# First mLSTM head of a hybrid encoder: its running maxima reach all partitions by transfers from DRAM, in place of products, a mask and copies

## What is computed

```python
b = jnp.cumsum(lfc, axis=-1)                               # log forget gates
dmat = jnp.where(tril, b[..., :, None] - b[..., None, :] + igc[..., None, :], -jnp.inf)
m_inter = b + m[..., None]
m_comb = jnp.maximum(jnp.max(dmat, axis=-1), m_inter)      # running maximum, the stabiliser
w_ts = jnp.exp(dmat - m_comb[..., None]) * jnp.einsum("bhtk,bhsk->bhts", qc, kc)
scale = jnp.exp(m_inter - m_comb)
num = jnp.einsum("bhts,bhsv->bhtv", w_ts, vc) + scale[..., None] * jnp.einsum("bhtk,bhvk->bhtv", qc, C)
den = jnp.sum(w_ts, axis=-1) + scale * jnp.einsum("bhtk,bhk->bht", qc, n)
h = num / jnp.maximum(jnp.abs(den), jnp.exp(-m_comb))[..., None]
```

## Time and profile before

| | before |
|---|---|
| median of 3 runs | 1865.18 us (1865.14 to 1869.9) |
| profiled execution, its own time | 1865.81 us |
| its span in the trace | 1864.0 us |
| granted TensorE clock, mean | 1.00 |
| PE busy | 1849.1 us, 99% |
| PE weight loads | 1741.0 us, 93% |
| VectorE | 1232.4 us, 66% |
| ScalarE | 880.2 us, 47% |
| GpSimd | 1161.8 us, 62% |
| SyncE's DMA queue | 349472 packets, 237.81 MB, 42.1% of 16 DMA engines |

### The profile page before, as it was taken

The page is one execution under the profiler, slowest core; times in us unless marked ns, Lnnn a source line. Parts: engine busy times, 40 slices in busy tenths (PEclk is TensorE's granted clock), DMA queues, the critical chain, the costliest instruction groups (busy, mean ns, idle before and its releaser), DMA issues.

```text
span 1864.0 us, 31419 instructions
## 1 busy us (share of the span) xinstructions
PE 1849.1 (99%) x10833; PEld 1741.0 (93%) x10833; DVE 1232.4 (66%) x2069; ACT 880.2 (47%) x1854; POOL 1161.8 (62%) x1533
## 2 busy tenths in 40 slices
PE   8999999999999999999999999999999999999999
PEld 8888888999999999999988888888889999999998
DVE  6756566768666766566866666666587575756663
ACT  6444343455444444455434444444465454444553
POOL 4543544468677878688843333333558788887885
PEclk9999999999999999999999999999999999999999
DMA  8789997549688877873466666654233535353534
GB/s 269 245 244 231 225 257 178 179 106 233 206 218 256 227 235 209 258 231 117 109 138 121 136 124 124 129 114 95 68 92 111 150 97 156 101 153 102 153 112 132
DMA packets 380153, 309.51 MB, mean 166 GB/s; under 512 B 14395, under 2 KB 322398, under 8 KB 379766
## 3 DMA queue, kind: packets, MB, share of 16 engines
q1 hardware_dynamic: 349472, 237.81, 42.1%
q0 software_dynamic: 28416, 69.21, 20.5%
q10 hardware_dynamic: 2134, 0.82, 0.2%
HBM read 302.16 MB, written 144.04 MB: 239 GB/s over the span
## 4 chain that ended last, share of the span: by engine, by line
PE 90%; DVE 6%; ACT 2%; issue 1%; DMA 1%; POOL 0%; ACTq 0%; DVEq 0%; SPq 0%; POOLq 0%
PE ps L974 50%; PE ps L884 26%; PE ps L1150 3%; PE ps L1307 3%; PE ps L1275 2%; PE ps L1297 1%; PE ps L1125 1%; DVE rstd L1497 1%; PE ps L1209 1%; PE ps L1159 1%; DVE sx L1549 0%; PE ps L1239 0%; DVE gt L1656 0%; PE ps L1027 0%; PE ps L1107 0%
## 5 line engine op out<-in xcount | busy, mean ns | idle before, releaser
L974 PE MATMUL ps<-sx,wh 128*128 128x400 f32 (+1 forms) x2044 | 530.4, 340 | 0.9 <-POOL wl L808 0.5
L808 POOL TENSOR_TENSOR wl<-raw,wh 128x256 fp32r<-128x256 f32 (+1 forms) x432 | 355.2, 853 | 99.7 <-ACT wh L2236 98.3
L774 POOL CAST wh<-raw 128x256 fp32r<-128x256 f32 x248 | 102.1, 453 | 454.2 <-PE ps L884 429.4
L974 PEld LDWEIGHTS ps<-sx,wh 128*128 128x128 f32 x2044 | 373.4, 188 | 2.8 <-ACT gt_first L2251 0.9
L974 PE MATMUL ps<-sx,wl 128*128 128x400 f32 (+1 forms) x1022 | 347.6, 340 | 0.0
L808 POOL TENSOR_TENSOR wl<-raws,wh 128x256 fp32r<-128x256 f32 x328 | 282.6, 906 | 82.8 <-ACT wh L2236 82.4
L1710 DVE TENSOR_TENSOR h<-h,ps 128x400 f32<-128x400 f32 (+1 forms) x280 | 154.5, 559 | 131.4 <-PE ps L974 131.2
L974 PE MATMUL ps<-fx,wh 128*128 128x400 f32 (+1 forms) x904 | 235.3, 341 | 0.1
L884 PE MATMUL ps<-xh,wh 128*128 128x512 f32 (+1 forms) x752 | 211.2, 357 | 0.0
L884 PE MATMUL ps<-xl,wh 128*128 128x512 f32 (+1 forms) x752 | 207.3, 349 | 0.0
L778 POOL TENSOR_TENSOR wl<-raw,wh 128x256 fp32r<-128x256 f32 x248 | 199.0, 831 | 5.1
(11 more groups left out here) (330 smaller groups left out, 3548.4 us busy)
## 6 DMA issues: line engine op xcount, KB each, us to landing
in_sums<-in_ffn_w_in_dram SPq DMA_DIRECT2D x16, 1536.0 KB, 10.6
raw<-in_sums SPq DMA_DIRECT2D x96, 256.0 KB, 3.1
in_sums<-in_ffn_w_in_dram SPq DMA_DIRECT2D x16, 1280.0 KB, 7.5
raw<-in_ffn_w_in_dram SPq DMA_DIRECT2D x80, 256.0 KB, 3.0
raws<-in_sums SPq DMA_DIRECT2D x80, 256.0 KB, 3.0
raw<-out_sums SPq DMA_DIRECT2D x120, 128.0 KB, 2.5
raws<-in_ffn_w_in_dram SPq DMA_DIRECT2D x52, 256.0 KB, 3.2
raw<-in_m_w_in_dram SPq DMA_DIRECT2D x24, 512.0 KB, 4.6
```

The source lines that it names most:

```text
L774: ins = pool.tensor_copy(wh[:, slot, c], raw[:, slot, c])
L808: ins = pool.tensor_tensor(slot_of(n, 1)[:, c], raw_of(n)[:, c], slot_of(n, 0)[:, c].bitcast(F32), ALU.subtract)
L974: mm = pe.matmul(product_bank(layer, s, j), slot_of(n, low_w)[:, k * P:(k + 1) * P], x, start=(j in OPENS and k + q == 0), stop=(k == tile ...
```

## The change

Head 0's maxima go the way of the others. The store is unchanged; behind it SyncE waits for its landing and issues the two broadcast reads of head 0 at once (`spread_maxima(0)`). The mask, the four products, ScalarE's two copies and their three semaphores are removed. VectorE waits for `maxima_in` 32 where it waited for `mrep_ready`, and for head hd in 1 to 3 on 32 more than before. `turn_ce` waits only for `gate_e`.

```diff
--- before.py
+++ after.py
@@ -523,7 +523,6 @@
         norm_sum, norm_root, rstd_ready = sem("norm_sum"), sem("norm_root"), sem("rstd_ready")
         vstep, astep, ones_set = sem("vstep"), sem("astep"), sem("ones_set")
         gates_done, gate_x, gate_soft, gate_m, gate_e = (sem(n) for n in ("gates_done", "gate_x", "gate_soft", "gate_m", "gate_e"))
-        mrow_masked, mrep_done, mrep_ready = sem("mrow_masked"), sem("mrep_done"), sem("mrep_ready")
         maxima_stored, maxima_in = sem("maxima_stored"), sem("maxima_in")
         ce_turned, ce_kept, ce_ready = sem("ce_turned"), sem("ce_kept"), sem("ce_ready")
         v_turned, vn_ready = sem("v_turned"), sem("vn_ready")
@@ -696,15 +695,19 @@
             sp.wait_ge(gate_m, 1)
             for d in range(2):
                 sp.dma_start(maxima_kept[d], mrow[64 * d:64 * d + M_HEADS, :]).then_inc(maxima_stored, 16)
+
+            def spread_maxima(hd):
+                for d in range(2):
+                    sp.dma_start(wk[:, 2 + d, :], maxima_kept[d, hd:hd + 1, :].to_broadcast([P, T])).then_inc(maxima_in, 16)
+
+            sp.wait_ge(maxima_stored, 32)
+            spread_maxima(0)
             for hd in range(1, M_HEADS):
                 for j in range(6):
                     n = MIX0 + hd * 6 + j
                     if j == 3:
-                        sp.wait_ge(maxima_stored, 32)
                         sp.wait_ge(e_ready, hd * NT)
-                        for d in range(2):
-                            sp.dma_start(wk[:, 2 + d, :], maxima_kept[d, hd:hd + 1, :].to_broadcast([P, T]))\
-                              .then_inc(maxima_in, 16)
+                        spread_maxima(hd)
                     weights(n, j % 2, mlstm_cols(hd, j))
                     sum_copies(n)
             for j in range(2):
@@ -1082,17 +1085,7 @@
 
             def mlstm_head(hd, n, first=False, last=False):
 
-                def repeat_m():
-
-                    pe.wait_ge(mrow_masked, 1)
-                    for d in range(2):
-                        for half in range(2):
-                            mm = pe.matmul(ps[:, 4 + 2 * d + half, 0:HT], ones[64 * d:64 * d + 32, :],
-                                           wk[64 * d:64 * d + 32, 4, half * HT:(half + 1) * HT], start=True, stop=True)
-                    mm.then_inc(mrep_done, 1)
-
                 def turn_ce():
-                    pe.wait_ge(mrep_ready, 2)
                     pe.wait_ge(gate_e, 2)
                     for i, (_, t0, tz) in enumerate(TILES):
                         mm = pe.transpose(flat(2)[0:tz, i * P:(i + 1) * P], cerow[:, t0:t0 + tz], ident)
@@ -1166,7 +1159,7 @@
 
                 run_block(n + 1, 1, 1, tokens="shared")
                 run_block(n + 2, 0, 0, tokens="shared")
-                run_block(n + 3, 1, 1, tokens="shared", between={2: [repeat_m], 4: [turn_ce], 7: call(turn_v, 0)} if first else {4: call(turn_v, 0)})
+                run_block(n + 3, 1, 1, tokens="shared", between={4: [turn_ce], 7: call(turn_v, 0)} if first else {4: call(turn_v, 0)})
                 tiles = {j + 2: call(scores, j) for j in OF_SEQ[0]}
                 tiles = {0: call(turn_v, 1), **tiles}
                 run_block(n + 4, 0, 0, tokens="shared", between=tiles)
@@ -1860,10 +1853,6 @@
 
                 if not first:
                     evacuate_shared(n, 0, wk[:, 0, :])
-                else:
-                    ve.wait_ge(gate_m, 1)
-                    ve.tensor_scalar(wk[:, 4, :], mrow[:, :], cst[:, ONEHOT:ONEHOT + 1], None, ALU.mult)\
-                      .then_inc(mrow_masked, 1)
                 evacuate_shared(*((n + 2, 0, wk[:, 6, :]) if first else (n + 1, 1, wk[:, 1, :])))
 
                 def query_key_lows():
@@ -1884,7 +1873,7 @@
                                          mask[0:tz, 0:tz], ALU.add).then_inc(diag_ready, 1)
 
                 if first:
-                    ve.wait_ge(mrep_ready, 2)
+                    ve.wait_ge(maxima_in, 32)
                     for j in (0, 1):
                         diagonals(j)
 
@@ -1900,7 +1889,7 @@
                 ve.tensor_copy(ce[:, :, :], ce_all[:, :, :, bass.ds(hd, 1)].rearrange("p i g c -> p i (g c)"))\
                   .then_inc(ce_ready, 1)
                 if not first:
-                    ve.wait_ge(maxima_in, hd * 32)
+                    ve.wait_ge(maxima_in, hd * 32 + 32)
                 for j in OF_SEQ[0][2 if first else 0:]:
                     diagonals(j)
                 if not first:
@@ -2543,10 +2532,6 @@
                 if not first:
                     query_key_high(n, 0)
                     query_key_high(n, 1)
-                else:
-                    sc.wait_ge(mrep_done, 1)
-                    for d in range(2):
-                        sc.activation(two(wk[:, 2 + d, :]), pair(2 + d), ACT.Copy).then_inc(mrep_ready, 1)
 
                 def values():
                     sc.wait_ge(v_turned, hd + 1)
```

## The result

The changed kernel takes 1872.22 us (median of 8 executions, 1871.36 to 1873.49), the kernel before beside it 1867.4 (8, 1865.14 to 1869.9). The ratio is 1.0029, 95% interval [1.002, 1.0037]: about 5.4 us slower, by the difference of the two medians 4.8. The forecast was 1872.0.

The account below looks back on a forecast made before the run. TensorE was taken to bound the kernel, with 90% of the last chain. Removing 1.55 us but adding a round trip, a 5.9 us stand and half clock gave +6.8 on the 1865.18 median: 1872.0 us, range 1867.0 to 1874.5.

Parts of the forecast that it names:

- case A: Stores wait behind the copy, PE stands near 6 us, clock falls: +6.2 to +7.3 us, chance 0.60.
- What it removes: Four products on PE's chain, 1.55 us; the VectorE multiply and ScalarE copies are off the chain, worth nothing.
- Step 1: On SyncE's queue: the maxima stores, issued at 56.15 behind the FFN weight copy, are done at 63.0.
- Step 2: SyncE issues the two spreads at 63.05 and 63.45; the second lands 5.1 us after issue, at 68.6.
- Step 3: VectorE makes four masked tiles (0.8 us) and the `ce_all` copies (0.5); PE starts `turn_v(0)` at 70.0.
- Steps 4 and 6: VectorE finishes block 3's evacuation at 72.2; ScalarE's first two tiles' exponentials end at 72.7, adding nothing.
- Step 5: PE stands 5.9 us ahead of `turn_v(0)`; at full clock `turn_v(1)` ends 4.7 us later than before.
- The clock: PE's stand brings 1.2 GHz through `turn_v(0)`, six matmuls and `turn_v(1)`: +6.8 us instead of +4.7.
- Queues: Head 1's weights and FFN copies wait behind SyncE's spreads; some 4 us late, covered more than twice.
- B: Same PE stand, but the clock holds or recovers soon: +4.7 to +5.3 us, chance 0.20.
- C: Stores land near 60.8 without a copy tail, PE stands 3.7 us: +2.5 us, 1867.7, chance 0.15.
- D: Not slower: stores pass the copy and the spread is quicker, 1863.6 to 1865.2 us, chance 0.05.

Follow-up runs that it names:

- the kernel before once more: The kernel before the change, unchanged, profiled a second time; median 1866.6 us, ratio 1.000 against the kernel before.
- the copy behind: Changed kernel with the 1280 KB FFN weight copy moved from ahead of the stores to behind head 0's spreads; ratio 1.0008 against the kernel before.
- PE kept busy: Changed kernel with 22 throwaway products put into TensorE's stand ahead of `turn_v(0)`; ratio 1.0016 against the kernel before.
- split held back: Changed kernel with GpSimd's split of block 5's weights held until the `ce_all` copies are made; ratio 1.0024 against the kernel before.

## Why the prediction was right, and where its steps were off

The mechanism was the one forecast, case A: the stores queue behind the copy, VectorE's list holds up `ce_kept` and the evacuation, PE stands, the clock falls. The rulers moved by 6.3 us against 6.8. Inside that sum two terms were wrong and nearly cancelled, and that is luck. So is the agreement of 1872.0 with 1872.22: the 6.8 was laid on a median of three runs that was 2.2 us lower than the 1867.4 measured beside the change, where the change itself came to 4.8 to 5.4 us.

- **What it removes**, 1.55 us: 1.7 measured.
- **Step 1, the stores done at 63.0, 6.9 us after issue**: wrong by 1.9 us. They released the spread after 4.9 to 5.4 us in each of the four kernels that have them behind the copy. What was mis-sized is the copy's own landing, taken from one execution: 8.5 us after its issue there, 7.0 in the kernel before once more, 6.5 to 6.9 in the four experiments that have it ahead, and in the changed kernel:

```profile
DMA to landing us min/median/max: 6.5/6.5/6.5
```

  The order was right: in each of the four the spread was issued 0.3 to 0.4 us after the copy had landed (here 53.29 + 6.5 = 59.8, and 60.20). That the queue is the cost stood: 2.4 us with the copy behind. The sum by the small transfer's fixed cost, +0.1, would have been wrong.
- **Step 2, 5.1 us from the second spread's issue to its landing**: 4.8 here, 4.5 to 5.3 over the experiments.
- **Step 3, four masks 0.8 us**: wrong by 1.6. They took 2.4, beside GpSimd's subtractions. The trace of before had a hint that I passed over. Of its first masks one took 0.82, and it is the one beside the last of GpSimd's subtractions, which end at 61.90 (timelines of VectorE and GpSimd, kernel before):

```profile
61.23 0.82 DVE L1883 TENSOR_TENSOR wt<-wk,maskb 128x128 f32<-128x128 f32 x1
61.97 0.28 DVE L1883 TENSOR_TENSOR wt<-wk,cst 128x128 f32<-128x128 f32 x1
```

```profile
57.55 4.35 POOL L778 TENSOR_TENSOR wl<-raw,wh 128x256 fp32r<-128x256 f32 x4
```

  My sum took the pace of the masks from 63.11 on, where GpSimd was quiet, and did not ask what GpSimd would be doing at 68.6.
- **Steps 4 and 6** held: the evacuation ended at 70.49 and ScalarE's exponentials at 71.1, both before `turn_v(1)` was through at half clock.
- **Step 5, a stand of 5.9 us**: 5.4, since 1.9 less and 1.6 more lie in it. The 4.7 at full clock is what PE kept busy shows: 30.6 − 26.4 = 4.2.
- **The clock**: +2.1 forecast over full clock, 2.2 measured. It lasted from before PE's restart to 73.7, nearly the end of `turn_v(1)`. The rule of the Trainium skill, "TensorE: Matmul & The Clock Gate", Part 1: The HAM clock gate, that an idle array goes to half clock, held here.
- **Queues**: head 1's weights were issued at 61.08 and GpSimd waited for PE, not for them; nothing was late there.

B is out in the profiled execution, and most likely in all: in each of the eight the mean clock is 0.997 or 0.998, while the kernel before has 0.999 or 1.000 in most of its own. C was nearly right on the stores (2.2 us earlier than my sum had them, 1.9 measured) and wrong on the time, because the slow masks filled what it gave back. Its price of +2.5 also took a stand of 3.7 us to cost nothing at the clock; the stand of 3.6 us in the kernel with the split held back brought 0.50. D failed on the stores.

The change against the median of three runs, 1865.18, was +7.0 and looked like more than it is: with more executions the kernel before has 1866.3 to 1867.4, and the ratio is 0.29%, on the edge of the 0.3% that I set for a difference.

The rest between the local 6.3 us and the 6.1 us of the spans is small things of both signs: the changed kernel's execution reached `gate_m` 0.9 us earlier and took 0.7 us more after the state reads. The kernel before once more took 1.5 us more there than in its first profile, so a difference of this size is found between executions of one kernel.

## What to carry to other kernels

A transfer through DRAM that replaces two microseconds of compute is a chain of three waits, the store behind whatever its queue holds, the load, and all that its reader has queued behind the wait; here that was 10 us against 1.7. Before taking such a path, move large copies behind it, release the store at the first moment the data is there, and put the wait in the reader's list at the last place that still serves, so that what others wait for goes first. With the three done here, and GpSimd's split kept away from the masks, the round trip fits, and only then is the compute saved.

## What the runs showed of the hardware

- **VectorE's adds keep GpSimd's pace.** VectorE's 128 x 128 adds with both inputs in SBUF start every 0.20 us with GpSimd quiet, every 0.40 beside its casts (0.40 each), and every 0.73 to 0.76 beside its subtractions (0.72 each). By these equal paces there is one add for one GpSimd instruction. The copies from PSUM in the same place are not slowed (0.47 us for four in each case). The Trainium skill, "SBUF — State Buffer", Who interferes with whom, says that a VectorE instruction with two SBUF inputs contends with a GpSimd one that reads SBUF, and that transfers don't contend with an engine; the runs agree with both.
- **The clock.** In the profiled executions, stands of 5.4, 3.8 and 3.6 us of PE in the middle of dense work brought 1.2 GHz; stands of 2.4 and 1.8 us did not. Of the stands near 13 us, those of 2.46 to 2.71 us (seven executions) did not, those of 2.73 to 3.02 (four) did. With 3.84 us the fall came some 0.7 us after PE had started again. So the price of a stand has a second part, 2.2 us here, and removing 1.8 us of a 5.4 us stand (split held back) did not save it in the profiled execution; the mean clocks of other executions of that kernel suggest that it can go either way.
- **The landing of a copy** of 1280 KB was 6.5 to 7.0 us after its issue in six executions and 8.5 in one. Why the last had a tail was not tried.
